# Fetching the V rows of two picks in one gather, and summing them as products on TensorE's two column halves

## The reference

```
def block(xb):                                   # 128 tokens
    q = (xb @ w_q).reshape(tb, PEER_HEADS, 2, PEER_D_KEY // 2)
    s = einsum('thcd,hckd->thck', q, sub_keys)   # 8 heads, 2 books of 128 keys
    top_s, top_i = top_k(s, 16)
    ...                                          # 16 best of the 256 sums, per head
    gate = softmax(best_s)
    u = u_tab[expert]
    act = gelu(einsum('td,thkd->thk', xb, u))
    w = gate * act
    return einsum('thk,thkd->td', w, v_tab[expert])
```

## Time and profile before

| | us |
|---|---|
| median of 3 runs | 3395.55 (3385.88 to 3400.23) |
| the profiled execution | 3410.71 |
| its span, first to last instruction | 3408.9 |
| PE busy, its products of v slots | 2680.2, 1794.8 |
| DVE busy, its u slots, its v slots | 2298.1, 1250.3, 185.0 |
| ACT busy, its diagonals | 733.0, 326.8 |
| POOL busy, gathers of u, of v | 2010.4, 995.9, 1009.0 |
| moved by DMA | 1185.46 MB, mean 348 GB/s |

### The profile page before, as it was taken

One profiled execution on the slowest core, in us unless ns is written; L12 is line 12 of the kernel. 1 busy time (PEld: TensorE's weight loads), 2 busy tenths in 40 slices (PEclk: granted clock), 3 DMA queues, 4 the chain that ended last, 5 costly groups with the idle time before them and its releaser, 6 DMA issues.

```text
span 3408.9 us, 26586 instructions
## 1 busy us (share of the span) xinstructions
PE 2680.2 (79%) x7136; PEld 1259.5 (37%) x7136; DVE 2298.1 (67%) x4976; ACT 733.0 (22%) x1629; POOL 2010.4 (59%) x2074
## 2 busy tenths in 40 slices
PE   7784578789898777888988777878998776666768
PEld 3454133344454332334444333334454322222223
DVE  1559966786578876777588876777478874455542
ACT  2321211232221121223222121223222111111111
POOL 0012576655566666666665667755666666666665
PEclk9796789889999899889999898889999999989889
DMA  5135899988999999998999999998999999999998
GB/s 184 72 140 193 281 381 407 407 325 327 387 392 371 368 358 407 407 377 325 395 406 371 361 365 408 406 376 296 384 407 385 343 358 369 374 356 383 375 355 327
DMA packets 351448, 1185.46 MB, mean 348 GB/s; under 512 B 37666, under 2 KB 38212, under 8 KB 351044
## 3 DMA queue, kind: packets, MB, share of 16 engines
q0 software_dynamic: 294912, 1073.87, 82.8%
q1 hardware_dynamic: 56388, 109.88, 8.7%
HBM read 1181.52 MB, written 2.10 MB: 347 GB/s over the span
## 4 chain that ended last, share of the span: by engine, by line
PE 26%; DVE 22%; issue 17%; POOL 17%; DMA 14%; another core or an unknown queue 4%; ACT 1%; DVEq 0%; POOLq 0%
PE peer_acc L1305 14%; DMA v_ring<-in_peer_v,experts 9%; POOL v_ring L513 9%; POOL u_ring L513 8%; DVE u_ring L1032 6%; DMA u_ring<-in_peer_u,experts 4%; PE act_bank L1091 3%; PE dve_bank L1091 2%; DVE work L798 2%; DVE work L787 1%; PE act_bank L1192 1%; DVE work L795 1%; DVE work L784 1%; DVE work L979 1%
## 5 line engine op out<-in xcount | busy, mean ns | idle before, releaser
L1305 PE MATMUL peer_acc<-v_ring,diag 128*128 128x512 f32 x3520 | 1794.8, 648 | 536.3 <-DMA v_ring<-in_peer_v,experts 411.0
L1032 DVE SCALAR_TENSOR_TENSOR u_ring<-u_ring,h_now 128x1024 f32<-128x1024 f32 x1024 | 1250.3, 1221 | 711.3 <-DMA u_ring<-in_peer_u,experts 546.8
L513 POOL DMA_INDIRECT u_ring<-in_peer_u,experts x1024 | 995.9, 973 | 725.7 <-issue 288.7
L513 POOL DMA_INDIRECT v_ring<-in_peer_v,experts x1024 | 1009.0, 985 | 658.1 <-PE peer_acc L1305 297.7
L1305 PEld LDWEIGHTS peer_acc<-v_ring,diag 128*128 128x128 f32 x3520 | 670.5, 203 | 1538.9 <-issue 757.0
L715 ACT ACTIVATE diag<-ident,wts 128x128 f32<-128x128 f32 x880 | 326.8, 396 | 1483.3 <-PE peer_acc L1305 794.1
L1091 PE MATMUL act_bank<-w_ring,hT 128*128 128x512 f32 x768 | 361.7, 619 | 8.8 <-ACT decay L682 4.2
L1042 DVE SCALAR_TENSOR_TENSOR xs<-v_ring,wts,xs 128x1024 f32<-128x1024 f32 x144 | 185.0, 1285 | 73.6 <-DMA v_ring<-in_peer_v,experts 62.4
L1091 PEld LDWEIGHTS act_bank<-w_ring,hT 128*128 128x128 f32 x768 | 155.7, 204 | 213.7 <-issue 208.9
L1178 PE MATMUL act_bank<-hT,w_ring 128*128 128x256 f32 x768 | 178.0, 388 | 31.5 <-ACT mix L555 31.5
L1178 PEld LDWEIGHTS act_bank<-hT,w_ring 128*128 128x128 f32 x768 | 149.5, 195 | 67.2 <-issue 47.7
(11 more groups left out here) (159 smaller groups left out, 1587.3 us busy)
## 6 DMA issues: line engine op xcount, KB each, us to landing
w_ring<-in_w_in SPq DMA_DIRECT2D x24, 2048.0 KB
w_ring<-in_peer_w_q SPq DMA_DIRECT2D x16, 2048.0 KB
w_ring<-in_w_out SPq DMA_DIRECT2D x8, 2048.0 KB
u_ring<-in_peer_u,experts POOLq DMA_INDIRECT x1024
v_ring<-in_peer_v,experts POOLq DMA_INDIRECT x1024
xs<-in_x SPq DMA_DIRECT2D x4, 512.0 KB, 7.5
keysT<-in_peer_sub_keys SPq DMA_DIRECT2D x2, 1024.0 KB
out<-xs SPq DMA_DIRECT2D x4, 512.0 KB
```

The lines of the kernel that those rows point to most:

```text
L513: pool.indirect_dma_start(ring[:, n % depth, :], None, table, bass.IndirectOffsetOnAxis(ap=experts[:, tile % TILES, e:e + 1], axis=0),).th ...
L1032: tell(nc.vector.scalar_tensor_tensor(out=row, in0=row, scalar=1.0, in1=h_now[:], op0=ALU.mult, op1=ALU.mult, accum_out=dots[:, c % 2, s:s ...
L1305: ins = nc.tensor.matmul(peer_acc[:, j * 512:(j + 1) * 512], diag[:, (v_count(c, s) - 1) % DIAGS, :], v_ring[:, n % V_RING, j * 512:(j + 1 ...
```

## The change

The v gather of a slot no longer fetches one pick for all 128 tokens. Slots go in pairs, pick q and pick q + 8 of a head. The even slot of a pair fetches both picks for tokens 0 to 63: partitions 0 to 63 hold pick q, partitions 64 to 127 pick q + 8. The odd slot fetches both for tokens 64 to 127. The number of gathers, their rows and bytes stay as they were. POOL takes the row numbers from a new array, `pair_experts`.

PE then needs, for each side (half of the tokens), one 128 x 64 matrix: two 64 x 64 diagonals on top of each other, with the weights of the two picks. Its product with the 128 fetched rows gives the sum of both picks for 64 tokens, in partitions 0 to 63 of `peer_acc` for the even slot and 64 to 127 for the odd one. PE works a pair at its odd slot: it waits for both gathers and the diagonals, then issues four products (two halves of 512 columns, two sides). Each side gives its buffer back with a semaphore of its own.

Half of the row numbers and weights have to go to the other half of the partitions. DVE writes those that stay (two operations of 64 partitions, in `route` and in `begin`), and ACT sends the others by DMA within SBUF: two DMAs per routing call (part 4 of the front, after `routed`), two per chunk (`move`, 10 slots before the chunk's first v slot). POOL waits for `experts_moved` before a call's first v gather, and ACT waits for `wts_moved` before a chunk's first diagonal. Diagonals are made 8 slots ahead instead of 7, in a ring of 6 pairs; gelu and weights move with them, to 13 and 11 slots before.

DVE has no v slots any more; `vector_slot` and what counts them is gone.

```diff
-DIAGS = 10
+DIAGS = 6
-V_EVERY = 8
+SIDE = P // 2
-D_AHEAD = 7
-GELU_BEFORE = D_AHEAD + 4
-WTS_BEFORE = D_AHEAD + 2
+D_AHEAD = 8
+GELU_BEFORE = D_AHEAD + 5
+WTS_BEFORE = D_AHEAD + 3
+MOVE_BEFORE = D_AHEAD + 2
...
+        def split(ap):
+            return ap.rearrange("p (h b q) -> p h b q", b=2, q=FEW)
...
 @block.gpsimd
+            link(pool.memset(ident2[:], 0.0))
+            for base in (0, -SIDE):
+                keep(ident2[:], ALU.not_equal, base, 1, [[-1, SIDE]], 1.0)
...
+                c, s = divmod(n, SLOTS)
+                if s == 0 and c % HPC == 0:
+                    pool.wait_ge(experts_moved, 32 * (call_of(c) + 1))
                 if n >= V_RING:
-                    old_c, old_s = divmod(n - V_RING, SLOTS)
-                    pool.wait_ge(v_added if by_vector(old_c, old_s) else v_used, v_count(old_c, old_s))
-                gather(v_rows, v_ring, V_RING, v_landed, *divmod(n, SLOTS))
+                    pool.wait_ge(v_used[n % 2], (n - V_RING) // 2 + 1)
+                gather(v_rows, v_ring, V_RING, v_landed, pair_experts, n, c % PH * TOPK + s % 2 * FEW + s // 2)
...
 @block.scalar
+                    if part == 4:
+                        j, i = divmod(n, HALF)
+                        heads = slice(j * HPC, (j + 1) * HPC)
+                        call = k * QJ * HALF + n
+                        act.wait_ge(routed, call + 1)
+                        if call:
+                            act.wait_ge(experts_moved, 32 * call)
+                        to, of = split(pair_experts[:, t0 + i, :]), split(experts[:, t0 + i, :])
+                        act.dma_start(to[SIDE:P, heads, 0, :], of[0:SIDE, heads, 1, :]).then_inc(experts_moved, 16)
+                        act.dma_start(to[0:SIDE, heads, 1, :], of[SIDE:P, heads, 0, :]).then_inc(experts_moved, 16)
...
+            def move(c):
+                act.wait_ge(wts_ready, c + 1)
+                to, of = pair_wts[:, c % 2, :], wts[:, c % 2, :]
+                act.dma_start(to[SIDE:P, 0:FEW], of[0:SIDE, FEW:SLOTS]).then_inc(wts_moved, 16)
+                act.dma_start(to[0:SIDE, FEW:SLOTS], of[SIDE:P, 0:FEW]).then_inc(wts_moved, 16)
...
             def diagonal(c, s):
-                if by_vector(c, s):
+                if s % 2:
                     return
-                act.wait_ge(wts_ready, c + 1)
-                n = v_count(c, s) - 1
-                if n >= DIAGS:
-                    act.wait_ge(v_used, n - DIAGS + 1)
-                nc.scalar.activation(diag[:, n % DIAGS, :], ident[:], ACT.Copy,
-                                     scale=wts[:, c % 2, s:s + 1]).then_inc(diag_ready, 1)
+                q = s // 2
+                if q == 0:
+                    act.wait_ge(wts_moved, 32 * (c + 1))
+                n = c * FEW + q
+                for side in range(2):
+                    if n >= DIAGS:
+                        act.wait_ge(v_used[side], n - DIAGS + 1)
+                    ins = nc.scalar.activation(diag[:, n % DIAGS, side * SIDE:(side + 1) * SIDE], ident2[:], ACT.Copy,
+                                               scale=pair_wts[:, c % 2, side * FEW + q:side * FEW + q + 1])
+                ins.then_inc(diag_ready, 1)
...
 @block.vector
+                    for b in range(2):
+                        rows = slice(b * SIDE, (b + 1) * SIDE)
+                        nc.vector.tensor_scalar_add(split(pair_experts[:, t, :])[rows, heads, b, :],
+                                                    split(sel[:, 0, :])[rows, :, b, :], float(l * EXPERTS))
...
+                for b in range(2):
+                    rows, cols = slice(b * SIDE, (b + 1) * SIDE), slice(b * FEW, (b + 1) * FEW)
+                    nc.vector.tensor_tensor(pair_wts[rows, c % 2, cols], acts[rows, c % 2, cols],
+                                            gates[rows, tile % TILES, head, cols], ALU.mult)
...
 @block.tensor
             def slot_v(c, s):
-                if by_vector(c, s):
+                if s % 2 == 0:
                     return
...
-                pe.wait_ge(v_landed[n % V_RING], 16 * (n // V_RING + 1))
-                pe.wait_ge(diag_ready, v_count(c, s))
+                for side in range(2):
+                    m = 2 * n + side
+                    pe.wait_ge(v_landed[m % V_RING], 16 * (m // V_RING + 1))
+                pe.wait_ge(diag_ready, n + 1)
                 for j in range(D // 512):
-                    ins = nc.tensor.matmul(peer_acc[:, j * 512:(j + 1) * 512], diag[:, (v_count(c, s) - 1) % DIAGS, :],
-                                           v_ring[:, n % V_RING, j * 512:(j + 1) * 512],
-                                           start=first, stop=last)
-                ins.then_inc(v_used, 1)
+                    for side in range(2):
+                        rows = slice(side * SIDE, (side + 1) * SIDE)
+                        ins = nc.tensor.matmul(peer_acc[rows, j * 512:(j + 1) * 512], diag[:, n % DIAGS, rows],
+                                               v_ring[:, (2 * n + side) % V_RING, j * 512:(j + 1) * 512],
+                                               start=(pair == 0), stop=(pair == PH * FEW - 1))
+                        if j == D // 512 - 1:
+                            ins.then_inc(v_used[side], 1)
```

More of the change, by code:

```diff
@@ L11 @@
 import math
-from itertools import accumulate
 from contextlib import ExitStack
@@ L358, in trunk, with interleave @@
             due_at[n] = range(first, done)
-        def vector_slot(n):
-            now = [kinds[part] for m in range(n - 1, n + 3) for part in due_at.get(m, ())]
-            if not now:
-                return n % V_EVERY == V_EVERY - 1
-            return "in" in now and n % 2 == 1
-        on_vector = [vector_slot(n) for n in range(CHUNKS * SLOTS)]
-        added_by = list(accumulate(int(mine) for mine in on_vector))
-        def by_vector(c, s):
-            return on_vector[c * SLOTS + s]
-        def v_count(c, s):
-            n = c * SLOTS + s
-            return added_by[n] if on_vector[n] else n + 1 - added_by[n]
-        def summed(slots):
-            return slots - added_by[slots - 1] if slots else 0
-        def interleave(front, ahead, slot_ahead, slot_now, before, begin, finish_tile):
+        def split(ap):
+            return ap.rearrange("p (h b q) -> p h b q", b=2, q=FEW)
+        def interleave(front, ahead, slot_ahead, slot_now, begins, finish_tile):
             parts = (None for k in range(FRONTS) for _ in front(k))
@@ L393, in interleave @@
                     finish_tile(c // PH - 1)
-                b, to = divmod(n + before, SLOTS)
-                if to == 0 and 0 <= b < CHUNKS:
-                    begin(b)
+                for before, begin in begins:
+                    b, to = divmod(n + before, SLOTS)
+                    if to == 0 and 0 <= b < CHUNKS:
+                        begin(b)
                 if 0 <= n + ahead < CHUNKS * SLOTS:
@@ L1034, in slot_u @@
                     op0=ALU.mult, op1=ALU.mult, accum_out=dots[:, c % 2, s:s + 1]), u_used, "u_used")
[L1036 to L1046 removed]
+            interleave(front, U_AHEAD, slot_u, lambda c, s: None, ((WTS_BEFORE, begin),), add_tile)
             add_tile(LAYERS * TILES - 1)
```

54 lines of the change are left out of this document (24 added, 30 removed).

## The result

The change makes the kernel slower: 3443.11 us (3441.74 to 3450.75) against 3391.02 us (3385.88 to 3400.23) for the kernel before on the same chip, ratio 1.016, 95% interval 1.0139 to 1.0181. On a second chip it was 1.015 (1.0126 to 1.0175). The forecast was 3386 us, a little faster than before. The time lies in the wide range of 3245 to 3480, just under rival B's 3450, but outside the forecast's own 3345 to 3430 and on the other side of the kernel before.

The account below looks back on a forecast made before the run. No engine was full: DMA traffic bound some stretches, PE and DVE were near full in others, and POOL's gather pace capped all. Terms summed to -10 us on 3410.7, 3401; less 15 for the median, 3386 us, range 3245 to 3480.

Parts of the forecast that it names:

- rival B: v ring: three pairs are too short, each hold costs 2.5 us; 3450 us, 3520 at worst; chance 0.22.
- hand-over: Moving row numbers and weights: DVE +4, DMA +5, ACT 0 us.
- relief of PE: Stretches with PE and DVE near full: halved v products save 54 us; bounds 0 and -130.
- v products, busy: PE: 512 pairs at about 2 us each, so busy near 1000 us instead of 1795.
- v ring: Even slot waits for its partner: 22 waits of POOL at 1.25 us, +28 us; bounds 0 and +160.
- end drain: Last 33 v gathers, after the last u gather: 1.64 us a slot, +6 us.
- DVE's slots: DVE: dropping its 144 v additions (185 us) gains 0, since they lay where the DMA was full.
- Rival C: PE: the two halves do not run together, giving 285 us more PE work; 3468 us; chance 0.06.
- ACT's wait for the moved weights: ACT before the diagonals: 0 us, covered by 5.6 and 22 us; bound +60; over 1 us each means wrong.
- ACT's wait for `routed`: ACT in front part 4, held to DVE's step: 0 us, bound +15 over 32 calls.
- The clock: PE in the last stretch may fall to 1.2 GHz more often, taking another 1.7 us off 2.9 us of slack.
- D: DVE is the bound at once and the ring is harmless; 3395 to 3410 us; chance 0.12.

Follow-up runs that it names:

- c1_v7u5: c1 with one buffer moved from the u ring to the v ring (V_RING 7, U_RING 5): 0.9988 of the kernel before.
- c2_v7u5: c2 with one buffer moved from the u ring to the v ring (V_RING 7, U_RING 5): 1.0023 of the kernel before.
- b_pair: Kernel before with every v slot on PE, worked in pairs at the odd slot with full-width products, nothing moved: 1.025 of the kernel before.
- a_nomove: Changed kernel without the hand-over: no moved row numbers or weights, no half-height DVE operations (sums other rows): 1.0034 of the kernel before.
- a_twice: Changed kernel with half weights in the diagonals and each pair's products issued twice: 1.0339 of the kernel before.
- a_single: Changed kernel with each side worked at its own slot and its buffer given back at once: 1.0016 of the kernel before.
- a_single_ring5: a_single with a v ring of 5 buffers instead of 6: 1.0157 of the kernel before.
- a_again: The changed kernel as it is, run again beside other variants on one chip: 1.015 of the kernel before.
- a_v7u5: Changed kernel with one buffer moved from the u ring to the v ring (V_RING 7, U_RING 5): 1.0033 of the kernel before.
- c2: a_single with c1's cheaper hand-over as well: 1.0008 of the kernel before.
- c1: Changed kernel, row numbers sent in the next call, full-height DVE writes, diagonals 6 slots ahead, weights still 10: 1.0091 of the kernel before.
- a_nowts: Changed kernel without the weights' move; row numbers still moved (half the weights belong to other tokens): 1.0143 of the kernel before.
- b_allpe: Kernel before with all 1024 v slots on PE, one at a time, none on DVE: 1.0014 of the kernel before.
- b_ring5: Kernel before with a v ring of 5 buffers instead of 6: 1.0131 of the kernel before.

## Why the prediction was wrong

The mechanism that the prediction named as speaking against the change, the even slot's late release, is what made it slower, together with the hand-over, whose delays use up the same slack. Any one of three edits takes most of the loss away: single sides (1.0016), a seventh buffer (1.0033), or no hand-over (1.0034). The forecast failed in the relief of PE, which was counted at -54 us and is worth about -12; that alone turns its -10 us into a loss. The ring and the hand-over were too small on top. What was forecast in each step, and what the runs gave:

| step | forecast, us | measured |
|---|---|---|
| v products, busy | near 1000 | 1312.8 |
| relief of PE | -54 | -12 (-4 to -19) |
| v ring | +28 | about +44 in the change, +28 with the cheaper hand-over |
| hand-over (DVE +4, DMA +5, ACT 0) | +9 | +15 to +39 |
| end drain | +6 | +4 to +8 |
| DVE's slots | 0 | +5 (-1 to +11) |

**Relief of PE: this term failed.** The 24.6% of the chain was read as a price: half the time of a link on the chain was to give half of its share back. c1_v7u5 against c2_v7u5 (0.9988 to 1.0023, rings alike, two chips) is the relief, with the even side's hold still in it: 0.35%, 12 us. PE's shorter products end sooner, but the gathers in 700 to 750 and 2300 to 2350 stayed 26 and 27. That the next thing in the loop (DVE's 41 to 44 of 50 us, the ring, the landing of the gathers) sets the pace at once is the likely reason; no run took these apart. Fewer products are worth more where the ring is short: 2.1% from b_pair to a_nomove, 1.8% from a_twice to the change. There each pair is also given back some 2 us sooner, and how much of that is PE's time and how much the ring's is not shown. The lower bound of the term, 0, was nearer than its value. What was right is that a pair takes the time of one slot. In a_single, four passes of one side, and in the change, eight passes of both, in the last stretch at the higher clock:

```profile
3006.40 1.93 PE L1318 MATMUL peer_acc<-v_ring,diag 128*64 128x512 f32 x4 [0.66 <-DMA v_ring<-in_peer_v,pair_experts]
```

```profile
3009.27 1.94 PE L1321 MATMUL peer_acc<-v_ring,diag 128*64 128x512 f32 x8 [1.44 <-issue]
```

The forecast's 1000 us assumed this everywhere; at half clock a pair is 3.6 to 3.7 us (1216.77 above), hence 1312.8. Rival C is out.

**The v ring: right mechanism, wrong size and place.** Three pairs of runs put the spacing of 2.5 us at 1.2 to 1.4%: a_single to a_single_ring5 (1.0016 to 1.0157), a_single to a_again (1.0016 to 1.015), a_v7u5 to a_again (1.0033 to 1.015, from two chips, with the price of the u buffer in it). Their mean, 1.3% of 3400 us, is 44 us. It is no constant: c2 to c1 gives 0.8% (28 us), c1_v7u5 to c1 1.0%, and without the hand-over a_nomove leaves 0.3% for pairs and relief together. The ring of five takes the spacing from every slot, the pairs from every second, and where pairs are compared with single sides what relief there is has been taken off already. The 28 us came from 22 waits in 600 us of the last stretch, at half a spacing each. But there the waits after are as before, 49.2 + 26.3 us then, and now

```profile
POOL v_ring L501 <- remote: 43.5, 15, 4.6
POOL v_ring L501 <- PE peer_acc L1321: 31.1, 13, 4.1
```

and gathers 832 to 992 took 452.2 us for 454.7 (457.4 on the second chip). What holds the releases in that stretch stays open. The slack counts where PE's own program is held up, at the beginnings of the fronts, in the first slots and at the end: there the pair's turn comes behind the front part, and a gap of 8 us became one of 15. The "steady pace is untouched" of the forecast holds. Its step that failed is that the holds come at random moments in the steady stretch: those that cost belong to the order of the program.

**The hand-over.** ACT's wait for the moved weights was costed at 0 by a cover of 5.6 + 22 us, with a bound of +60. The wait was not 0: ACT stood 114.0 us for the landing, 29 times, up to 5.7 us. That is 1.8 us for each of the 64 chunks, over the 1 us that the prediction had named as a sign of being wrong. ACT's timeline in an early chunk:

```profile
399.14 0.67 ACTq L716 DMA_DIRECT2D pair_wts<-wts  x1
399.84 0.62 ACTq L717 DMA_DIRECT2D pair_wts<-wts  x1
400.51 0.59 ACT L729 ACTIVATE diag<-ident,pair_wts 128x64 f32<-128x64 f32 x2 [11.87 <-issue]
404.39 1.54 ACT L729 ACTIVATE diag<-ident,pair_wts 128x64 f32<-128x64 f32 x6 [3.30 <-DMA pair_wts<-wts]
```

Two slots in program order are 5.6 us only where ACT is on time. Here it is late: it issues both DMAs, makes the diagonals of one more pair, and 2.0 us after the first issue began it stands for 3.3 us. Yet a_nowts can't tell this wait's price from nothing; the row numbers, with ACT's wait for `routed` (bound +15), were the dearer half (about 0.6%, 20 us), where the prediction's bounds were the other way round. Removed together, a_nomove: 1.2%. With the longer ring the cheaper version gives 0.45%, in single sides 0.1%: the hand-over delays ACT and through it PE, and costs only as far as the ring has no slack for it. That PE is the way by which ACT's delay reaches the ring is argued from this pattern, not followed in a trace. So the terms were not additive, and the sum treated them so. At their measured sizes, and the hand-over as with the longer ring, they come, with b_allpe's 5, to -12 + 44 + 15 + 5 = +52 us (the end drain is in the 44); the change cost 51 to 54 (1.5 and 1.6%). That this closes so well is partly luck, each term being known to some 7 us and the 44 resting on which pair of runs is taken.

**The clock.** PE did fall to 1.2 GHz more often: with the two levels 1.2 and 2.4 GHz, a mean of 0.821 for 0.916 is an estimated 1230 us of the span at the lower one, where it was 570. The Trainium skill (TensorE: Matmul & The Clock Gate, section HAM oscillation — how this bites in real kernels) holds that thin products between DMA waits let the clock drop again and again; the trace agrees as to the clock (0.69 in 2900 to 2950). That this made rival B more likely is not borne out: a_v7u5 and a_nomove run at 0.82 within 0.35% of before, and a_single_ring5 loses as much at 0.939.

**The rivals.** B (3450 to 3520) was nearest in mechanism, and its sign of POOL's v waits above 400 us came (450.0); its DMA share below 0.9 in the last stretch did not (0.97). D was right that relief buys next to nothing, and took the ring to be harmless. Other signs: the DMA share in 700 to 800 was 0.85, not near 1.0, and the last v gathers were 1.74 us apart for a forecast of 1.6 (1.54 before), so the end drain came out as costed. The chances gave slower 0.35 and B 0.22. That was too little: POOL already waited 372 us for a ring with 5.4 us of mean slack, and b_ring5 shows what one spacing less costs such a ring.

## What to carry to other kernels

Before two steps are fused to save an engine's time, ask what each of them gives back and when: for a buffer held one spacing longer the ring is one buffer shorter, and if the producer already waits for the ring, that price is real while the saved time may buy nothing. A share on the chain of waits is an upper bound for a gain, not a price. Look for the cost of lost slack where the consumer's program is held up by other work in its order, not in the steady stretches, and don't add up terms that draw on the same slack. The total of the producer's waits is a poor guide: it was 465 us in a kernel that lost 0.3% and 450 in one that lost 1.6%.

## What was not expected of the hardware

Products with 64 columns on the two column halves overlapped in full, eight passes in 1.94 us as four in 1.93, although both sides alternate in the program. A granted clock of 0.82 instead of 0.92 did not show in this gather-fed kernel: at 0.82 it ran at 1.0033 (a_v7u5) and 0.9988 (c1_v7u5) of the time before. A DMA of 2 KB from ACT within SBUF took ACT 0.47 or 0.62 us to issue (first and second of a pair, medians), and its landing held ACT back for up to 5.7 us beside full gather queues; the 19456 packets themselves took 0.3% of the DMA engines' time (10 us), near to the 10 us that were estimated.
